# Eighteen instead of sixteen gate tiles in the seven-product projection, and the attention stage's slots dealt anew

## What is computed

```
u = rms_norm(x, norm_pre);  p = u @ w_in            # 2048 -> 9744 columns:
#   attention q 1024, k 256, v 256, gate 1024 | gla q 512, k 512, v 1024, gate 1024 | rank 16 | merge gates 2048 + 2048
branch A: chunk-banded attention (chunk 64, window 128, ALiBi, sinks), times silu(gate), @ w_branch_attn
branch B: gated linear attention (4 heads, 128 x 256 state, per-token decay), rms_norm, times silu(gate), @ w_branch_gla
h = x + rms_norm((sigmoid(g_A) * y_A + sigmoid(g_B) * y_B) @ w_out, norm_post)
```

## Time and profile before

| | |
|---|---|
| time, median of 3 runs (lowest to highest) | 2827.69 us (2826.9 to 2828.65) |
| the profiled execution: time, span in the trace | 2828.88 us, 2827.1 us |
| PE busy | 2736.5 us (97%), 20860 matmuls |
| DVE, ACT, POOL busy | 2125.1 (75%), 1209.3 (43%), 80.0 us (3%) |
| projection (PE L2217 up to) | 1348 us |
| attention stage | 1348 to 2050 us |
| branch stage, output stage | 2050 to 2416 us, 2416 to 2827 us |

### The profile page before, as it was taken

One profiled execution on the slowest core, in us unless ns is written; L12 is line 12 of the kernel. 1 busy time (PEld: TensorE's weight loads), 2 busy tenths in 40 slices (PEclk: granted clock), 3 DMA queues, 4 the chain that ended last, 5 costly groups with the idle time before them and its releaser, 6 DMA issues. The chain is left out here.

```text
span 2827.1 us, 52027 instructions
## 1 busy us (share of the span) xinstructions
PE 2736.5 (97%) x20860; PEld 2595.6 (92%) x20860; DVE 2125.1 (75%) x3375; ACT 1209.3 (43%) x1972; POOL 80.0 (3%) x55
## 2 busy tenths in 40 slices
PE   7999999998999999999999999999899989999996
PEld 7999999998999999999777887877799989999996
DVE  7999778778787877877777777777676877655556
ACT  5344333445354333344556566565522322342331
POOL 0221000000000000000000000000000000000001
PEclk9999999999999999999999999999999999999998
DMA  4455433435344343344656666565634456555564
GB/s 153 165 187 186 143 122 121 135 124 200 102 143 135 121 135 123 121 133 131 193 168 179 184 181 180 163 195 159 213 138 177 171 209 233 165 173 182 188 193 140
DMA packets 234187, 456.95 MB, mean 162 GB/s; under 512 B 23905, under 2 KB 139745, under 8 KB 233073
## 3 DMA queue, kind: packets, MB, share of 16 engines
q1 hardware_dynamic: 233968, 453.91, 49.8%
HBM read 365.90 MB, written 88.47 MB: 161 GB/s over the span
## 5 line engine op out<-in xcount | busy, mean ns | idle before, releaser
L2217 PE MATMUL bank<-th,w_hi 128*128 128x272 f32 x2360 | 686.0, 291 | 3.2 <-DVE w_lo L1458 2.2
L2217 PE MATMUL bank<-tl,w_hi 128*128 128x272 f32 x2360 | 681.9, 289 | 0.0
L2217 PE MATMUL bank<-th,w_lo 128*128 128x272 f32 x2360 | 681.3, 289 | 0.0
L1445 DVE TENSOR_TENSOR w_lo<-w_raw,w_hi 128x1024 fp32r<-128x1024 f32 x224 | 273.8, 1222 | 235.0 <-ACT w_hi L1011 234.6
L2217 PEld LDWEIGHTS bank<-th,w_hi 128*128 128x128 f32 x2360 | 444.4, 188 | 6.3 <-issue 3.1
L2217 PEld LDWEIGHTS bank<-tl,w_hi 128*128 128x128 f32 x2360 | 444.5, 188 | 1.0 <-issue 1.0
L2217 PEld LDWEIGHTS bank<-th,w_lo 128*128 128x128 f32 x2360 | 444.1, 188 | 0.0
L1026 ACT ACTIVATE w_hi<-w_more 128x1024 fp32r<-128x1024 f32 x236 | 250.2, 1060 | 424.6 <-PE bank L2217 222.0
L1011 ACT ACTIVATE w_hi<-w_raw 128x1024 fp32r<-128x1024 f32 x224 | 236.8, 1057 | 367.5 <-PE bank L2531 239.1
L1458 DVE TENSOR_TENSOR w_lo<-w_more,w_hi 128x1024 fp32r<-128x1024 f32 x236 | 297.6, 1261 | 93.0 <-ACT w_hi L1026 92.8
L2195 PE MATMUL bank<-uh,w_hi 128*128 128x272 f32 x1024 | 316.0, 309 | 13.3 <-DVE w_lo L1445 8.5
(11 more groups left out here) (287 smaller groups left out, 5644.4 us busy)
## 6 DMA issues: line engine op xcount, KB each, us to landing
w_raw<-in_w_tiles SPq DMA_DIRECT2D x344, 512.0 KB, 4.1
w_more<-in_w_tiles SPq DMA_DIRECT2D x120, 512.0 KB, 3.6
p_scratch<-stage SPq DMA_DIRECT2D x44, 544.0 KB, 3.0
gl<-p_scratch SPq DMA_DIRECT2D x24, 512.0 KB, 5.6
w_pair<-in_w_tiles SPq DMA_DIRECT2D x9, 1024.0 KB, 8.7
gate_scratch<-stage SPq DMA_DIRECT2D x16, 544.0 KB, 3.0
gate_scratch<-stage SPq DMA_DIRECT2D x64, 136.0 KB, 4.2
gate_even<-gate_scratch SPq DMA_DIRECT2D x8, 1088.0 KB, 6.2
```

The source lines that it names most:

```text
L1445: dve.tensor_tensor(w_lo[:, h], w_raw[:, h], w_hi[:, h].bitcast(f32), ALU.subtract).then_inc(s_wlo, 1)
L2217: ins = pe.matmul(out[:, 0:GAW], wt[:, k], ut[:, k], start=start and k == 0 and i == 0, stop=stop and k == HK - 1 and i == 2, skip_group_c ...
```

## The change

`N_EARLY` goes from 16 to 18, so one more pair of gate tiles goes through the projection: 31 pairs, 62 mixes instead of 60. `N_LATE` becomes 14, with 56 units and 224 slots in the attention stage; the turns come at slots 56, 112 and 168, which is slot 20 of rounds 2, 4 and 6. `SLOTS` and `JOINED` are dealt anew: rounds 0 to 8 have 18, 18, 28, 28, 28, 28, 25, 24 and 15 slots, the end 12 as before. With 18 slots steps 14, 16, 18 and 21 to 25 are joined to those before them; with 25 step 21, with 24 steps 21 and 25. With 28 slots only steps 3 and 6 have an empty slot behind them, where 32 had six (steps 3, 6, 17, 18, 19, 20). In round 8, steps 0 and 1, 6 and 7, and 12 to 14 share a slot besides.

`RING_AT` turns the ring of three so that its last product (now number 434 instead of 420) again ends in the same buffer; it is added wherever the ring is indexed.

```diff
-N_EARLY = 16
+N_EARLY = 18
 RING = 3
+RING_AT = -MIX_Q % RING
-SLOTS = (21, 21, 32, 32, 32, 32, 27, 27, 20)
-JOINED = (21, 25, 24, 14, 16, 18)
+SLOTS = (18, 18, 28, 28, 28, 28, 25, 24, 15)
+JOINED = (21, 25, 24, 14, 16, 18, 23, 22)
-                act.activation(ring_hi[done % RING], w_src_of[RAW_OF[q]], ACT.Copy).then_inc(s_phi, 1)
+                act.activation(ring_hi[(done + RING_AT) % RING], w_src_of[RAW_OF[q]], ACT.Copy).then_inc(s_phi, 1)
...
```

More of the change, by code:

```diff
@@ L1035, in hi_first @@
                 ge(act, s_mp, e + 1 if e == 3 else 0)
-                act.activation(ring_hi[(3 + e) % RING], w_src_of[(0, 2, 1, 3)[e]], ACT.Copy).then_inc(s_phi, 4 if e == 0 else 1)
+                act.activation(ring_hi[(3 + e + RING_AT) % RING], w_src_of[(0, 2, 1, 3)[e]], ACT.Copy).then_inc(s_phi, 4 if e == 0 else 1)
             def squares(*pieces):
@@ L1457, in lo_mix @@
                 dve.wait_ge(s_phi, done + 1)
-                dve.tensor_tensor(ring_lo[done % RING], w_src_of[RAW_OF[q]], ring_hi[done % RING].bitcast(f32), ALU.subtract).then_inc(s_plo, 1)
+                dve.tensor_tensor(ring_lo[(done + RING_AT) % RING], w_src_of[RAW_OF[q]], ring_hi[(done + RING_AT) % RING].bitcast(f32), ALU.subtract).then_inc(s_plo, 1)
             def lo_ahead(n, q):
@@ L1501, in lo_first @@
                 dve.wait_ge(s_phi, 4 + e)
-                dve.tensor_tensor(ring_lo[(3 + e) % RING], w_src_of[(0, 2, 1, 3)[e]], ring_hi[(3 + e) % RING].bitcast(f32),
+                dve.tensor_tensor(ring_lo[(3 + e + RING_AT) % RING], w_src_of[(0, 2, 1, 3)[e]], ring_hi[(3 + e + RING_AT) % RING].bitcast(f32),
                                   ALU.subtract).then_inc(s_plo, 4 if e == 0 else 1)
@@ L2259, in first_product @@
                 pe.wait_ge(s_plo, 4 + e)
-                hi_w, lo_w = ring_hi[(3 + e) % RING], ring_lo[(3 + e) % RING]
+                hi_w, lo_w = ring_hi[(3 + e + RING_AT) % RING], ring_lo[(3 + e + RING_AT) % RING]
                 for k in range(HK):
@@ L2300, in _ @@
                         pe.wait_ge(s_post, 6 * n + 4)
-                    split_product(bank[(0, 1, 0, 1, 2, 1, 2)[q]], ring_hi[(N_Q * n + q) % RING], ring_lo[(N_Q * n + q) % RING],
+                    split_product(bank[(0, 1, 0, 1, 2, 1, 2)[q]], ring_hi[(N_Q * n + q + RING_AT) % RING], ring_lo[(N_Q * n + q + RING_AT) % RING],
                                   tok_hi[q], tok_lo[q], q in (0, 1, 4), q in (2, 5, 6))
```

## The result

| | before | after |
|---|---|---|
| median of 8 runs (lowest to highest) | 2828.21 us (2826.71 to 2829.54) | 2837.77 us (2834.95 to 2840.55) |
| ratio, 95% interval | | 1.0033 [1.0022, 1.0044] |
| profiled execution | 2828.88 us | 2837.63 us |

What follows compares the result with a forecast made beforehand. PE's matmuls were taken to bound the projection and nearly fill the attention stage; 43.7 us saved less 42.4 added gave 1.3 us faster, 2826.4 us against 2827.69, with a range of 2819.5 to 2834 and 0.68 for within 5.7 us.

Steps and rivals of the forecast that it cites:

- the clock: Attention stage: new waits of 2 to 3 us may or may not cost 1.7 us each through a lower granted clock.
- The even chance: Rounds 0 and 6: a clock fall behind the wait taken as even odds, 0.4 to 0.8 us in their figures.
- The joined steps 17 and 18: Rounds 0 and 1: removing the slot between them gives 1.7 less 0.7 us wait for state updates, 1.0 us saved.
- the parity of steps 14 and 16: Round 1: these joined steps move to round 0's slot parity, where they cost less by some 1.3 us.
- The turns: Rounds 2 and 4: turn on step 18 without empty slots around it costs 4.0 us; savings 4.9 and 4.4 us.
- The two mixes: Projection: two added mixes at 21.2 us each add 42.4 us on PE.
- the named upper bound of 7.8: Rounds 3 and 5: 6.0 us saved each, at most 7.8 if their 1.0 us of idle time also went.
- the chain at the end of rounds 0 and 1: End of linear attention, silu, gmean, groot, os: some 4.2 us, with PE idle some 2.3 us in both rounds.
- Rival (b): Turn rounds and joined steps: the in-order DVE queue sets them, 34.6 us come out, 7.8 us slower, 2835.5; chance 0.12.
- Rival (a): Attention stage: all removed slots save full worth, 52.2 us, without new waits; 9.8 us faster, 2817.9; chance 0.20.

Runs made afterwards that it cites:

- f1_fill: Changed kernel plus idle matmuls where PE waits, without start flag, in the bank of the unit in progress: 2826.64 us, 0.9991 to the kernel before.
- e2_room: Changed kernel with the two empty slots of rounds 2 and 4 behind steps 17 and 18 instead of 3 and 6: 2834.63 us, 1.0021.
- e1: Changed kernel with steps 17 and 18 of rounds 0 and 1 apart again and step 1 joined to step 0: 2835.79 us, 1.0026.
- e4: Changed kernel without the remaking of tokens at the turns, including its loads and waits: 2814.77 us, 0.9952 to the kernel before.
- f3: Changed kernel with idle matmuls in rounds 2 and 4 only, at steps 18 and 20: 2833.19 us, 1.0016 to the kernel before.
- h1: Changed kernel, no idle matmuls, with DVE's ul in the turns writing 8 of 272 columns: 2828.86 us, 0.9997 to the kernel before.
- h2: Changed kernel, no idle matmuls, with ACT's uh in the turns writing 8 of 272 columns: 2831.58 us, 1.0009 to the kernel before.
- f4: Kernel before the change, without the remaking of tokens at the turns: 2819.8 us, 0.9969 to the kernel before.
- e3_fill: Changed kernel plus idle matmuls where PE waits, with start flag, into unused columns of one gate bank: 2825.68 us, 0.9992 to the kernel before.

## Why the prediction was wrong

| us | r0 | r1 | r2 | r3 | r4 | r5 | r6 | r7 | r8 | last 12 | sum |
|---|---|---|---|---|---|---|---|---|---|---|---|
| forecast | 61.3 | 61.5 | 80.9 | 75.9 | 79.9 | 75.9 | 75.8 | 68.6 | 49.3 | 28.6 | 657.7 |
| after | 63.5 | 64.9 | 82.4 | 74.2 | 82.8 | 74.2 | 76.2 | 68.5 | 51.8 | 28.2 | 666.7 |
| f1_fill | 61.9 | 63.3 | 79.5 | 74.2 | 79.7 | 74.2 | 75.4 | 69.3 | 50.4 | 27.9 | 655.8 |

**The step that failed: the clock.** The sum held 0.4 to 0.8 us for it in the figures of rounds 0 and 6, from a chance of 1.7 us behind two waits. Seven more stretches came than before, at 1.5 us each by the pairs above, and holding the clock gave 10.9 us (666.7 - 655.8). The price of one was nearly right; the number was not. I counted only the waits at the ends of rounds and in round 6, and had priced the new waits at steps 18 and 20 and in round 8 by their length alone. The even chance was read from single waits in the earlier trace rows, 0.98 and 2.27 us long, without looking at what PE does around them. I also left out a second stretch that before has, in its last 12 slots, behind waits of 2.25 and 1.83 us, neither longer than the 2.27 us that had none (view of before, columns as in the earlier trace rows):

```profile
2034.00:2037.50 3.50, 3.50 (x18) 3.50 (x18) 3.02 (x4) 0.44 (x2) 0.00 (x0) 0.53 0.82 211
```

The text named the limit itself: wrong "if the granted clock falls in more than three new places". It fell at six (1436.4, 1501.2, 1583.2, 1740.2, 1900.6, 1992.8), and two of them lasted twice 3.4 us. The Trainium skill's rule (TensorE: Matmul & The Clock Gate, "HAM oscillation — how this bites in real kernels") was weighed there at 4 us for four waits. The trace of after agrees that waits drop the clock, with eight stretches, but not that each one does: 2.24 and 2.23 us at the ends of rounds 0 and 1 had none behind them.

**The joined steps 17 and 18** were priced at 0.7 us of wait; after shows 1.01 + 0.94 in round 0 and 1.36 + 0.94 in round 1. The 6.5 us for round 1 were also more than the terms beside them give (3.1 + 1.0 + 1.3 = 5.4, and 0.85 for half a stretch). With the clock held, rounds 0 and 1 are still 0.6 and 1.8 us over the forecast. In round 1 the 1.3 us that the parity of steps 14 and 16 was to bring is not to be seen; no run tests that part alone. Round 8 is 1.1 over with the clock held: steps 6 and 7 together wait 1.73 us for pT, for which its 0.7 was too little.

**The turns.** 4.0 us each stood for them in rounds 2 and 4, which were to save 4.9 and 4.4 us, with bounds of 2 to 7. They saved 3.4 and 1.5, the second below its bound. With no turn the two rounds take 74.1 and 74.2 us, so a turn costs 8.3 and 8.6, more than the 6 that the text named as a sign of being wrong: 5.3 and 5.6 of idle time, somewhat over the 4.0, and the clock for the rest. With the clock held (f1_fill) they save 6.3 and 4.6, near the forecast and inside the bounds. The mechanism was half right: I named the waits of ul for ACT but priced DVE's surplus of work alone, and the timeline shows a chain in which ACT waits for DVE and DVE for ACT. Shortening DVE's part from 7.0 to 2.8 us leaves 3.2 of 5.3 us of idle time in round 2. Round 6 was forecast at 75.8 and took 76.2 us, with the 2.85 us wait for ul where "over 3 us" stood.

**Right.** The two mixes cost 41.5 us to the start of the stage (42.4 forecast), and twenty of them still take 424.2 us. Rounds 3 and 5 nearly reached the named upper bound of 7.8: 7.7 us less each, not 6.0, as their early waits went too. Those 3.4 us covered what the joined steps cost too much, so that the ten rounds with the clock held come to 1.9 us under their forecast sum. Round 7, the last 12 slots and the chain at the end of rounds 0 and 1 came as forecast. That chain, in round 1 of after:

```profile
1513.35 0.17 DVE L1830 TENSOR_SCALAR gmean<-gmean 128x4 f32<-128x4 f32 x1
...
1513.59 1.01 POOL L1410 TENSOR_TENSOR groot<-gmean,minus_half 128x4 f32<-128x4 f32 x1 [63.96 <-DVE gmean L1830]
...
1514.63 1.57 ACT L1229 ACTIVATE os<-bank,groot 128x256 f32<-128x256 f32 x4 [1.61 <-POOL groot L1410]
```

It ends at 1516.2, and the last output product at 1512.15: 4.1 us, 4.2 forecast.

**The rivals.** Rival (b) gave 34.6 us for what the stage returns, and 34.7 came. That is chance for the larger part: with the clock held 45.6 us come out, 1.4 us a slot, and its in-order queue fits the idle time of the turns and the joined steps but not the 10.9 us. Rival (a) would have needed 52 us; f1_fill shows that it misses even with a held clock. A rival was missing: that several short waits, none of them dear by itself, each may drop the clock.

## What to carry to other kernels

When work that fills gaps on PE is taken away, count the new waits of 1 to 3 us and price each with its own chance of a fall of the clock, read where you can from the same place in a trace and not from the length alone: the same wait dropped the clock nearly always in one place and hardly ever in another (below). Where PE has to wait anyway, idle matmuls into unused columns of a bank can hold the clock (11 us here), but they are a floor for the time at that place and have to be shorter than the wait. A filler slot behind a step can cost more than its matmuls (7.7 us went with four in rounds 3 and 5, at 1.5 us of matmuls each). A turn that goes through two in-order engines was cheaper where empty slots stood around it (9 us before, 23 after), though two of them put back alone did little (e2_room).

## What the runs showed of the hardware

- The length of a wait did not decide alone on the clock. Over the profiled executions in which these waits stand with no idle matmuls at them (runs by their first two characters):

| wait on PE | runs | half clock behind it |
|---|---|---|
| 2.24, 2.23 us, ends of rounds 0 and 1 | after, e1, e2, e4, f3, h1, h2 | 1 of 14 (round 1 of e1) |
| 2.38 us, end of round 1 | before, f4 | 2 of 2 |
| 1.0 or 1.4 and 0.94 us, step 18 of rounds 0 and 1 | after, e2, e4, f3, h1, h2 | 12 of 12 |
| 1.0 or 1.5 and 0.94 us, step 18 of rounds 2 and 4 | after, e1, h2 | 1 of 6 (round 2 of e1) |
| 1.73 us, step 7 of round 8 | after, e1, e2, e4, f3, h1, h2 | 7 of 7 |

- The same wait also came out both ways in one kernel: 2.45 and 2.46 us in rounds 2 and 4 of h2_uh_short_plain, and 1.01 with 0.94 us in its rounds 0 and 2. What decides was not found.
- Every such stretch in the stage lasted 3.4 or 6.8 us and cost about 1.5 us for 3.4 us (7.6 us for five in e4_noturn's comparison; 75.89 against 74.37 us in h2_uh_short_plain), a little under the half of the stretch, 1.7 us, that I had taken.
- With idle matmuls that set the start flag, into columns of a bank that nobody uses, the outputs h were off by 5 and 7% (e3_fill); without the flag, and in the bank of the unit in progress, they were not disturbed (f1_fill). Flag and choice of bank changed together, so no run here separates the two.
